# Two preparation steps of a cross-attention stage moved within a hand-written order (one core)

## The chip, the cores and the metric

The kernel runs on one core of a Trainium2 chip. The metric is the device time of one execution in microseconds (us), the median over several executions. Lower is better.

## The reference

The reference is a transformer of fourteen stages in float32 on 256 tokens of width 1024. Eight stages are gated feed-forward layers, four are token mixers of different kinds, and two are cross-attentions to a memory of 256 rows. Only the two cross-attentions (kind "xa", layers 0 and 1) are touched here:

```python
def memory_cross_attention(h, m, w_q, w_kv, q_gain, k_gain, w_o):
    q = rms_norm((h @ w_q).reshape(b, s, X_HEADS, X_HEAD_DIM), q_gain)
    kv = (m @ w_kv).reshape(b, m.shape[1], 2, X_HEADS, X_HEAD_DIM)
    k = rms_norm(kv[:, :, 0], k_gain)
    v = kv[:, :, 1]
    sc = jnp.einsum('bqhd,bkhd->bhqk', q, k).astype(jnp.float32) * (X_HEAD_DIM ** -0.5)
    p = jax.nn.softmax(sc, axis=-1).astype(v.dtype)
    o = jnp.einsum('bhqk,bkhd->bqhd', p, v).reshape(b, s, X_HEADS * X_HEAD_DIM)
    return o @ w_o
```

It is called with `h = rms_norm(x, xa_norm)` and `m = rms_norm(mem, xa_mem_norm)`. There are 4 heads of width 256.

## The kernel before, in words

**Tiles and precision.** All weights come as one stream of 829 tiles of 128x1024 in the order of use. SyncE loads them into four raw buffers (L421); a raw buffer is free once the tile in it is split. ScalarE casts a tile to its high part (`w_hi`, L1053), VectorE subtracts to get the low part (`w_lo`, L1487), and TensorE forms a product from three matmuls (high by high, high by low, low by high, L461). A projection tile ("w") is 8 chunks of 3 matmuls, 24 in all. The split parts lie in a ring of six, so TensorE can have several tiles ready ahead of it. Activations are split in the same way: a "high" on ScalarE (L1074) and a "low" on VectorE (L1514), chunk by chunk (8 chunks of 128 rows by 256 tokens).

**One list, five engines.** Each engine walks the same list of units from `before(kind, layer)`, and then, within the attention, one short list per group from `between(kind, layer)`. Each engine does its own share of a unit, strictly in the list's order, and engines meet only at semaphores. The units that matter here:

- `mh` c: the high (ScalarE) and low (VectorE) parts of chunks c and c+1 of the memory, written to the buffer "b". TensorE does nothing for it.
- `start` (kind "trio"): three query tiles at once, chunk by chunk, then the sum of squares of x; ScalarE takes its square root, VectorE the reciprocal `rstd_x` (L1506) and the three evacuations (L1732).
- `w` / `wk`: one projection tile. TensorE multiplies; VectorE evacuates it (L1716) and then splits the weight tile four places ahead; ScalarE casts that tile. `wk(0)` is the first tile that reads the memory's parts: TensorE waits before each of its 8 chunks for that chunk's low part.
- `hs`: ScalarE squares two evacuated tiles (L1241). `hn`: TensorE sums these squares over the head (it waits for `hs`), ScalarE takes the root (L1259), VectorE the reciprocal (L1774) and scales the two tiles (L1780, L1782).
- `vh`: half of a value tile; ScalarE evacuates after the second half (L1191).
- `att`: the attention's first step. On TensorE it is the scores of group 0, on VectorE their maximum (L1818, L1819), on ScalarE their exponentials (L1285).

In the attention, ScalarE does for each group g first the exponentials of group g+1, then the units of the group's list, then the copy of the transposed probabilities (L1297). TensorE does first the scores of group g+1 or g+2, then the same units, then the transposes (L823):

```python
                exps(0)
                yield
                for g in range(len(groups)):
                    if g + 1 < len(groups):
                        exps(g + 1)
                    for u in fill[g]:
                        unit(*u)
```

Before the change the list of an "xa" stage has the four `mh` units first, ahead of the trio. The squares of the last key head, `hs(*k(3))`, stand in `before` between `wk(7)` and the first half value tile, and its `hn` stands in the first list of `between`.

Of the kernel before, what the change touches and what calls it, by code (L numbers as in the profile page):

```python
# [141 lines left out]
def build(nc, stream_d, x_d, mem_d, vec_d, con_d, biasa_d, biasc_d, heads_d, out_d, stages=STAGES):  # L142
    total = sum(TILES[s] for s, _ in stages)
    with ExitStack() as ctx:
        def sb(name, shape, dt=F32):
            return ctx.enter_context(nc.sbuf_tensor(name, shape, dt))
# [14 lines left out]
        v = sb("v", [P, 2, D])  # L161
# [157 lines left out]
        def before(kind, layer):  # L319
            def hs(name, i, a, b):  # L320
                return ("hs", name, i, layer, a, b)

            def hn(name, i, a, b):
                return ("hn", name, i, layer, a, b)

            def w(k, *where):
                return ("w", "a", "x", k, *where)

            def start(*tiles):
                return ("trio", "a", "x", tiles, (T_BANK, 0, 2) if kind == "xa" else None)  # L330
            def hb(name, *pairs):
                return ("hb", name, layer, pairs)

            def vh(i, half):
                return ("vh", "a" if kind == "odd" or kind == "even" else "b", "x" if kind in ("odd", "even") else "m", v, i, half)
            if kind == "even":
                return [start(0, 1, 2), w(3, 0), hs("evq", 0, 0, 1), w(4, 1), ("col", "x"), hn("evq", 0, 0, 1),
                        hs("evq", 1, 2, 3), vh(0, 0), hn("evq", 1, 2, 3), hs("evk", 0, 4, 4), vh(0, 1), hn("evk", 0, 4, 4),
                        ("mem",), vh(1, 0), hb("evq", (0, 0, 1), (1, 2, 3)), vh(1, 1), hb("evk", (0, 4, 4)), ("stat", "m"),
                        vh(2, 0), ("col", "m"), ("att",), vh(2, 1)]  # L340
            if kind == "odd":
                def q(i):
                    return ("odq", i, 2 * i, 2 * i + 1)

                def k(i):
                    return ("odk", i, 2 * i + 8, 2 * i + 9)
                return [start(0, 1, 2), w(3, 0), hs(*q(0)), w(8, 1), ("col", "x"), w(9), hs(*q(1)), hn(*q(0)), w(10),
                        hn(*q(1)), w(11), hs(*k(0)), hb("odq", q(0)[1:], q(1)[1:]), w(4), hs(*k(1)), hn(*k(0)), w(5),
                        hn(*k(1)), w(6), hs(*q(2)), hb("odk", k(0)[1:], k(1)[1:]), w(7), w(12), ("att",), hs(*q(3)), hn(*q(2)), w(13),
                        hn(*q(3)), w(14), hs(*k(2)), hb("odq", q(2)[1:], q(3)[1:]), w(15), vh(0, 0), hs(*k(3)), hn(*k(2))]  # L350
            if kind == "xa":
                def q(i):
                    return ("xaq", i, 8 + 2 * i, 9 + 2 * i)

                def k(i):
                    return ("xak", i, 2 * i, 2 * i + 1)

                def wk(i):
                    return ("w", "b", "m", i)
                return [*(("mh", c, layer) for c in (0, 2, 4, 6)), start(8, 9, 10), w(11, 1), hs(*q(0)), w(12, 3), hs(*q(1)),  # L360
                        w(13), hn(*q(0)), w(14), hn(*q(1)), hs(*q(2)), w(15), wk(0), hn(*q(2)),
                        hs(*q(3)), wk(1), wk(2), hn(*q(3)), hs(*k(0)), wk(3), wk(4), hn(*k(0)), hs(*k(1)), wk(5), wk(6),
                        hs(*k(2)), hn(*k(1)), ("att",), wk(7), hs(*k(3)), vh(0, 0), hn(*k(2))]
            return ([start(0, 1, 48), w(2, 0), w(3, 1), ("col", "x")]
                    + [w(k) for k in range(4, 12)] + [("att",)] + [w(k) for k in range(12, 16)] + [("v", "a", "x", v, i) for i in range(4)])

        def between(kind, layer):

            if kind == "even":
                return [[("w", "a", "x", 5 + 2 * g), ("w", "a", "x", 6 + 2 * g)] for g in range(4)]  # L370
            if kind == "odd":
                out = [[("vh", "a", "x", v, (g + 1) // 2, (g + 1) % 2)] for g in range(7)] + [[]]
                out[0].append(("hn", "odk", 3, layer, 14, 15))
                out[1].insert(0, ("hb", "odk", layer, ((2, 12, 13), (3, 14, 15))))
                return out
            if kind == "xa":
                k3 = ("xak", 3, layer, 6, 7)
                return [[("vh", "b", "m", v, 0, 1), ("hn", *k3)]] + [[("v", "b", "m", v, g)] for g in range(1, 4)]
            rest = [("w", "a", "x", 16 + k) for k in range(8)] + [("v", "a", "x", v2, i) for i in range(4)]
            rest += [("w", "a", "x", 24 + k) for k in range(8)]  # L380
            return [rest[2 * g:2 * g + 2] for g in range(4)] + [rest[8 + 3 * g:11 + 3 * g] for g in range(4)]
# [62 lines left out]
        def _(pe):  # L444
# [311 lines left out]
            def attention(kind, layer):  # L756
# [4 lines left out]
                last_group = len(groups) - 1  # L761
                base = dict((s, t.so_far(s)) for s in (max_done, exp_done, p_ready, a_ready, pt_ready, o_lo, o_out))
                fill = between(kind, layer)

                def scores(g):
# [202 lines left out]
            def mixer(kind, layer):  # L968
# [4 lines left out]
                for u in before(kind, layer):  # L973
                    unit(*u)
# [53 lines left out]
        def _(act):  # L1028
# [233 lines left out]
            def attention(kind, layer):  # L1262
# [3 lines left out]
                cols = 2 * T if kind == "xa" else T + P  # L1266
                base = dict((s, t.so_far(s)) for s in (max_done, recip_done, tr_done, o_done))
                fill = between(kind, layer)
                into = "a" if kind == "xa" else "b"

# [114 lines left out]
            def mixer(kind, layer, following):  # L1385
# [4 lines left out]
                for u in before(kind, layer):  # L1390
                    unit(*u)
                    if kind == "mix" and u[0] == "w" and u[3] == 5:
                        gates()
                    if u[0] == "mem":
                        act.wait_ge(mem_loaded, 32)
                        for c in range(C):
                            square(c, mem[:, c, :])
# [72 lines left out]
        def _(dve):  # L1470
# [332 lines left out]
            def attention(kind, layer):  # L1803
                groups = groups_of(kind)
                nm = len(groups[0]["maps"])
                n_sets = 1 if kind in ("xa", "mix") else 2
                base = dict((s, t.so_far(s)) for s in (s_mm, exp_done, tr_done, o_hi, a_part, recip_done))
                fill = between(kind, layer)
                into = "a" if kind == "xa" else "b"

# [188 lines left out]
            def mixer(kind, layer, following):  # L1999
# [3 lines left out]
                for u in before(kind, layer):  # L2003
                    unit(*u)
                    if u[0] == "mem":
                        add_squares()
                    if kind == "mix" and u[0] == "w" and u[3] in (4, 8, 10):
                        gates(layer, (4, 8, 10).index(u[3]))
# [345 lines left out]
```

## Time and profile before

| what | value |
|---|---|
| median of three runs | 2628.57 us (2623.86 to 2634.04) |
| the profiled execution: its own time | 2623.86 us |
| its span in the profile | 2622.1 us |
| TensorE (PE) busy | 2545.0 us, 97% |
| VectorE (DVE) busy | 1802.4 us, 69% |
| ScalarE (ACT) busy | 1396.5 us, 53% |
| GpSimd (POOL) busy | 190.6 us, 7% |
| bytes moved | 445.89 MB, mean 170 GB/s |

PE is TensorE's matmuls, PEld its weight loads, PEclk the clock that TensorE was granted as a share of full speed. A timeline row gives the start in us from the span's start, the duration, the engine, the line of the kernel, the operation and its operands; in brackets stands the idle time of the engine just ahead of it and what ended that.

### The profile page before, as it was taken

What the parts mean: (1) busy time and instruction counts of PE and PEld (TensorE: products, weight loads), DVE (VectorE), ACT (ScalarE), POOL (GpSimd) and SP (SyncE); (2) the same over time, 40 slices, a digit from 0 to 9 for tenths busy, and PEclk for the clock granted to TensorE, in tenths of its full rate; (3) what the DMA queues carried; (4) which work ended last, traced back from release to release, by engine and by line L of the source; (5) the groups of instructions that cost most, each with busy time, mean ns of one, the idle gap of its engine ahead of it and who ended that gap; (6) DMA issues with size and microseconds to landing.
All of it is one profiled execution on the core that took longest, in us unless ns stands there. A gap on an engine that the chain in (4) does not pass through costs nothing.

```text
span 2622.1 us, 56431 instructions
## 1 busy us (share of the span) xinstructions
PE 2545.0 (97%) x21370; PEld 2468.5 (94%) x21370; DVE 1802.4 (69%) x2868; ACT 1396.5 (53%) x2232; POOL 190.6 (7%) x265
## 2 busy tenths in 40 slices
PE   8999799999999999999999999999999989999998
PEld 8998699999998899999998998989989989989998
DVE  6667686667667585767667657786686676676865
ACT  5456556445445655545445555654454465555543
POOL 0001001000000201000000250000000005300000
PEclk9999899999999999999999999999999999999999
DMA  7664244765564344655654543545545545335553
GB/s 270 208 192 137 81 145 157 234 211 188 195 194 155 105 164 142 201 193 180 203 193 147 182 146 113 169 161 185 184 161 192 193 147 174 129 115 176 175 193 113
DMA packets 122826, 445.89 MB, mean 170 GB/s; under 512 B 13688, under 2 KB 14712, under 8 KB 122688
## 3 DMA queue, kind: packets, MB, share of 16 engines
q1 hardware_dynamic: 120816, 436.79, 50.8%
q0 software_dynamic: 1872, 7.17, 0.8%
q8 instruction: 98, 1.61, 0.3%
q14 instruction: 40, 0.33, 0.0%
HBM read 442.86 MB, written 1.05 MB: 169 GB/s over the span
## 4 chain that ended last, share of the span: by engine, by line
PE 92%; DVE 5%; ACT 2%; issue 1%; DMA 0%; SPq 0%; DVEq 0%; ACTq 0%
PE bank L461 91%; DVE w_lo L1487 1%; PE bank L823 1%; DVE x L1558 1%; ACT w_hi L1053 1%; DVE z L1598 0%; DVE rstd_x L1506 0%; DVE x L1602 0%; DVE rstd_m L1553 0%; DVE score L1547 0%; DVE a L1514 0%; DMA raw<-in_stream_dram 0%; ACT score L1285 0%; DVE score L1538 0%; DVE z L1902 0%
## 5 line engine op out<-in xcount | busy, mean ns | idle before, releaser
L461 PE MATMUL bank<-a,w_hi 128*128 128x256 f32 x7472 | 1311.2, 280 | 37.6 <-DVE a L1514 28.0
L461 PEld LDWEIGHTS bank<-a,w_hi 128*128 128x128 f32 x7472 | 1137.1, 189 | 52.1 <-issue 47.4
L1487 DVE TENSOR_TENSOR w_lo<-raw,w_hi 128x1024 fp32r<-128x1024 f32 x829 | 1012.6, 1225 | 212.4 <-ACT w_hi L1053 210.8
L461 PE MATMUL bank<-a,w_lo 128*128 128x256 f32 x3736 | 1039.0, 278 | 0.0
L1053 ACT CAST w_hi<-raw 128x1024 fp32r<-128x1024 f32 x829 | 842.3, 1045 | 57.3 <-DMA raw<-in_stream_dram 53.8
L461 PE MATMUL bank<-b,w_hi 128*128 128x256 f32 x4800 | 839.3, 278 | 1.0 <-DVE b L1487 1.0
L461 PEld LDWEIGHTS bank<-b,w_hi 128*128 128x128 f32 x4800 | 726.8, 188 | 8.5 <-issue 3.6
L461 PEld LDWEIGHTS bank<-a,w_lo 128*128 128x128 f32 x3736 | 707.7, 189 | 0.0
L461 PE MATMUL bank<-b,w_lo 128*128 128x256 f32 x2400 | 664.9, 277 | 0.0
L461 PEld LDWEIGHTS bank<-b,w_lo 128*128 128x128 f32 x2400 | 451.4, 188 | 0.0
L1113 ACT CAST b<-hmid 128x256 fp32r<-128x256 f32 x132 | 53.8, 407 | 401.0 <-PE bank L461 389.7
L1625 DVE TENSOR_TENSOR hmid<-bank,rstd_x 128x256 f32<-128x256 f32 x168 | 71.2, 424 | 163.6 <-PE bank L461 163.5
L1109 ACT ACTIVATE sil<-sil 128x256 f32<-128x256 f32 x176 | 73.6, 418 | 145.7 <-DVE sil L1620 145.7
L1487 DVE TENSOR_TENSOR b<-hmid,b 128x256 fp32r<-128x256 f32 x132 | 56.0, 425 | 128.3 <-ACT b L1113 128.3
L461 PE MATMUL bank<-w_hi,a 128*128 128x256 f32 x736 | 130.7, 281 | 0.0
L2163 POOL TENSOR_SCALAR score<-score,rr 128x128 f32<-128x128 f32 (+1 forms) x96 | 44.5, 479 | 1114.7 <-DVE rr L1842 817.5
L461 PEld LDWEIGHTS bank<-w_hi,a 128*128 128x128 f32 x736 | 111.9, 188 | 3.4 <-issue 2.5
L1716 DVE TENSOR_TENSOR z<-bank,rstd_x 128x256 f32<-128x256 f32 x125 | 52.8, 422 | 79.0 <-PE bank L461 78.4
L461 PE MATMUL bank<-w_lo,a 128*128 128x256 f32 x368 | 102.2, 278 | 0.0
L1113 ACT CAST a<-hmid 128x256 fp32r<-128x256 f32 x44 | 17.9, 407 | 136.1 <-PE bank L461 132.5
L1639 DVE TENSOR_TENSOR hmid<-sil,hmid 128x256 f32<-128x256 f32 x176 | 74.8, 425 | 5.7
L1620 DVE TENSOR_TENSOR sil<-bank,rstd_x 128x256 f32<-128x256 f32 x160 | 67.8, 424 | 12.7 <-PE bank L461 2.8
(193 smaller groups left out, 1897.1 us busy)
## 6 DMA issues: line engine op xcount, KB each, us to landing
raw<-in_stream_dram SPq DMA_DIRECT2D x829, 512.0 KB, 3.7
z<-in_biasc_dram POOLq DMA_DIRECT2D x6, 512.0 KB, 4.9
z<-in_biasa_dram POOLq DMA_DIRECT2D x3, 512.0 KB, 4.7
x<-in_x_dram SPq DMA_DIRECT2D x2, 512.0 KB, 8.0
v<-in_mem_dram POOLq DMA_DIRECT2D x2, 512.0 KB, 5.9
out_dram<-x SPq DMA_DIRECT2D x8, 128.0 KB, 1.8
con<-in_con_dram POOLq DMA_DIRECT2D x1, 912.0 KB, 6.6
vec<-in_vec_dram POOLq DMA_DIRECT2D x1, 417.0 KB, 5.6
```

Source lines behind the costliest of these rows:

```text
L461: return nc.tensor.matmul(out, lhsT, rhs, start=start, stop=stop, skip_group_check=shared)
L823: last = nc.tensor.transpose(out[:, col:col + P], p[:, src:src + P], ident)
L1053: nc.scalar.copy(w_hi[:, slot, :], raw[:, raw_slot, :]).then_inc(hi_split, 1)
L1109: nc.scalar.activation(sil[:, jj, :], sil[:, jj, :], ACT.Silu).then_inc(silu_done, 1)
L1113: nc.scalar.copy(high_of["b"][:, jj, :], hmid[:, jj, :]).then_inc(hhi_done, 1)
L1487: return nc.vector.tensor_tensor(out, a, hi.bitcast(F32), ALU.subtract)
L1558: ins = nc.vector.tensor_tensor(x[:, c, :], x[:, c, :], rstd["m"][:, :], ALU.mult)
L1620: nc.vector.tensor_tensor(sil[:, j % 2, :], gate_up_of(j, after_mixer)[0], r, ALU.mult)\
L1625: nc.vector.tensor_tensor(hmid[:, j % 2, :], gate_up_of(j, after_mixer)[1], r, ALU.mult)\
L1639: nc.vector.tensor_tensor(hmid[:, jj, :], sil[:, jj, :], hmid[:, jj, :], ALU.mult)\
L1716: nc.vector.tensor_tensor(z[:, tile, :], out[:, 0:T], rstd[norm][:, :], ALU.mult).then_inc(w_evac, 1)
L2163: last = nc.gpsimd.tensor_scalar(p, p, rr[:, k, b:b + 1], 1.0, ALU.mult, ALU.mult)
```

## The change

Three edits in the lists, for both "xa" stages. The four `mh` units leave the front of `before`: the first now stands behind `hn(*q(0))`, the second behind `hs(*q(2))`, the third and fourth behind `w(15)`, directly ahead of `wk(0)`. And `hs(*k(3))` leaves `before` and becomes the first unit of the first list of `between`, so that on ScalarE it comes behind the exponentials of group 1.

```diff
-                return [*(("mh", c, layer) for c in (0, 2, 4, 6)), start(8, 9, 10), w(11, 1), hs(*q(0)), w(12, 3), hs(*q(1)),
-                        w(13), hn(*q(0)), w(14), hn(*q(1)), hs(*q(2)), w(15), wk(0), hn(*q(2)),
+                return [start(8, 9, 10), w(11, 1), hs(*q(0)), w(12, 3), hs(*q(1)), w(13), hn(*q(0)), ("mh", 0, layer), w(14),
+                        hn(*q(1)), hs(*q(2)), ("mh", 2, layer), w(15), ("mh", 4, layer), ("mh", 6, layer), wk(0), hn(*q(2)),
                         hs(*q(3)), wk(1), wk(2), hn(*q(3)), hs(*k(0)), wk(3), wk(4), hn(*k(0)), hs(*k(1)), wk(5), wk(6),
-                        hs(*k(2)), hn(*k(1)), ("att",), wk(7), hs(*k(3)), vh(0, 0), hn(*k(2))]
+                        hs(*k(2)), hn(*k(1)), ("att",), wk(7), vh(0, 0), hn(*k(2))]
...
             if kind == "xa":
                 k3 = ("xak", 3, layer, 6, 7)
-                return [[("vh", "b", "m", v, 0, 1), ("hn", *k3)]] + [[("v", "b", "m", v, g)] for g in range(1, 4)]
+                return [[("hs", *k3), ("vh", "b", "m", v, 0, 1), ("hn", *k3)]] + [[("v", "b", "m", v, g)] for g in range(1, 4)]
```

## Rows read from the trace of the kernel before

**Rows 1.** The page, part 1: busy time of each engine over the span.

```profile
PE 2545.0 (97%) x21370; PEld 2468.5 (94%) x21370; DVE 1802.4 (69%) x2868; ACT 1396.5 (53%) x2232; POOL 190.6 (7%) x265
```

**Rows 2.** Stretches of the two xa stages: busy time of each engine, granted clock, DMA.

```profile
324.50:385.40 60.90, 60.90 (x488) 59.39 (x487) 52.43 (x74) 33.32 (x51) 0.94 (x2) 1.00 0.48 156
926.40:987.20 60.80, 60.80 (x487) 59.33 (x486) 52.47 (x74) 33.50 (x51) 0.94 (x2) 1.00 0.47 157
```

**Rows 3.** The waits of TensorE over the whole span: total, times, longest.

```profile
PE bank L461 <- DVE w_lo L1487: 9.2, 8, 1.8
```

**Rows 4.** Timeline of VectorE, front of the first xa stage.

```profile
327.52 3.25 DVE L1514 SCALAR_TENSOR_TENSOR b<-v,vec,b 128x256 fp32r<-128x256 f32 x8
330.69 1.22 DVE L1487 TENSOR_TENSOR w_lo<-raw,w_hi 128x1024 fp32r<-128x1024 f32 x1
334.71 1.75 DVE L1506 RECIPROCAL rstd_x<-rstd_x 128x256 f32<-128x256 f32 x1 [2.80 <-ACT rstd_x L1068]
```

**Rows 5.** Timeline of ScalarE, same stage: memory highs, a late cast.

```profile
326.04 3.29 ACT L1074 ACTIVATE b<-v,vec 128x256 fp32r<-128x256 f32 x8
...
343.49 1.05 ACT L1053 CAST w_hi<-raw 128x1024 fp32r<-128x1024 f32 x1 [2.58 <-DMA raw<-in_stream_dram]
```

**Rows 6.** Timeline of VectorE, first xa stage, up to wk(0)'s evacuation.

```profile
344.58 1.23 DVE L1487 TENSOR_TENSOR w_lo<-raw,w_hi 128x1024 fp32r<-128x1024 f32 x1 [1.46 <-ACT w_hi L1053]
...
348.30 0.42 DVE L1716 TENSOR_TENSOR z<-bank,rstd_x 128x256 f32<-128x256 f32 x1
...
352.35 0.42 DVE L1716 TENSOR_TENSOR z<-bank,rstd_x 128x256 f32<-128x256 f32 x1
...
353.81 0.42 DVE L1716 TENSOR_TENSOR z<-bank,rstd_m 128x256 f32<-128x256 f32 x1
```

**Rows 7.** Timeline of VectorE, the same place of the second xa stage.

```profile
944.88 1.23 DVE L1487 TENSOR_TENSOR w_lo<-raw,w_hi 128x1024 fp32r<-128x1024 f32 x1
...
952.64 0.42 DVE L1716 TENSOR_TENSOR z<-bank,rstd_x 128x256 f32<-128x256 f32 x1
```

**Rows 8.** DMA issues at 338.56, then at 940.38: size, us to landing.

```profile
raw<-in_stream_dram SPq DMA_DIRECT2D x1, 512.0 KB, 4.9
...
raw<-in_stream_dram SPq DMA_DIRECT2D x1, 512.0 KB, 3.4
```

**Rows 9.** Timeline of TensorE: wk(0)'s first matmuls, hn(q2)'s, hn(k3)'s, hn(q2)'s in the second stage.

```profile
349.38 0.39 PE L461 MATMUL bank<-b,w_hi 128*128 128x256 f32 x2
...
352.10 1.03 PE L461 MATMUL bank<-sil,con 128*128 128x256 f32 x4
...
384.53 1.02 PE L461 MATMUL bank<-hmid,con 128*128 128x256 f32 x4
...
953.93 1.03 PE L461 MATMUL bank<-sil,con 128*128 128x256 f32 x4
```

**Rows 10.** Chain that ended last at 301.83: VectorE's end to TensorE's start.

```profile
301.83 0.14 issue
```

**Rows 11.** Timeline of ScalarE around hs(k3), first xa stage.

```profile
378.09 0.64 ACT L1241 ACTIVATE hmid<-z 128x512 f32<-128x512 f32 x1
...
379.69 1.28 ACT L1259 ACT_TABLE_LOAD   x1
...
385.33 0.47 ACT L1285 ACTIVATE score<-bank,nmx 128x256 f32<-128x256 f32 x1 [2.57 <-DVE nmx L1819]
...
386.24 1.04 ACT L1053 CAST w_hi<-raw 128x1024 fp32r<-128x1024 f32 x1
```

**Rows 12.** Timeline of VectorE: the reciprocal of hn(k2), first xa stage.

```profile
381.49 1.75 DVE L1774 RECIPROCAL rt<-rt 128x256 f32<-128x256 f32 x1 [0.56 <-ACT rt L1259]
```

**Rows 13.** Timeline of TensorE after two pauses of other stages.

```profile
865.32 0.52 PE L823 MATMUL bank<-con,score 128*128 128x128 f32 x3 [1.64 <-ACT pt L1297]
...
1721.26 0.76 PE L461 MATMUL bank<-a,w_hi 128*128 128x256 f32 x2 [3.81 <-DVE a L1514]
```

**Rows 14.** Stretches behind these pauses: columns as in rows 2.

```profile
868.00:871.00 3.00, 3.00 (x15) 2.77 (x14) 1.66 (x4) 2.99 (x10) 0.35 (x1) 0.50 0.00 0
...
1721.20:1724.20 3.00, 2.94 (x14) 2.97 (x15) 3.00 (x9) 2.06 (x7) 0.00 (x0) 0.50 0.00 0
```

## The prediction

> **What bounds the kernel now.** I read the page first: TensorE is busy for 97% of the span, so a change pays only where TensorE stands still, and costs wherever it makes TensorE stand still [rows 1]. Next came the stretches of the two stages that the change touches. From 324.5 us to the point where the attention's first transposes begin, TensorE is busy 60.90 of 60.90 us in the first stage and 60.80 of 60.80 us in the second, at the full granted clock [rows 2]. The view of waits, asked for 322 to 426 us and for 924 to 1028 us, lists no wait of TensorE at all. So the old order costs TensorE nothing, and there is no idle time there for the new order to win back. The question is only whether the new order makes TensorE wait. For that I read the timelines of VectorE and ScalarE, because the moved units run on these two alone, and laid them beside TensorE's.
>
> **Edit 1, what it removes.** At the front, eight highs on ScalarE take 3.29 us [rows 5] and eight lows on VectorE 3.25 us [rows 4]. The next instruction starts 3.17 us after the first low, so one low takes up 3.17 / 8 = 0.40 us of VectorE and lasts 3.25 - 7 x 0.40 = 0.48 us from start to result. TensorE is in the 72 matmuls of the trio then. Behind the lows VectorE does one weight split and then waits 2.80 us for the root, which waits for TensorE's own sum of squares [rows 4]. The 3.2 us that the edit frees therefore end in that wait: it becomes about 6 us, and everything after it starts when it did. The removal is worth nothing; its cover was the trio.
>
> **Edit 1, what it adds.** The same lows now stand in the stretch between `hn(q0)` and `wk(0)`, where VectorE has no pause. In the first stage its last wait is the one before 344.58 (1.46 us, for a late cast), and from there to 353.81 it goes from one instruction to the next [rows 6]. It is also already behind TensorE: `w(15)` is evacuated at 352.35 [rows 6], although TensorE left that tile for `wk(0)` at 349.38 [rows 9]. Today this lag of 3.0 us hurts nobody, since `wk(0)` needs nothing that VectorE makes in it. After the edit it does, because the last four memory chunks come behind that evacuation. Step by step, first stage:
>
> - `mh` 0 behind `hn(q0)` pushes the evacuation of `w(14)` from 348.30 to 349.10. Chunks 0 and 1 are ready just in time for TensorE at 349.38.
> - `mh` 2 behind `hn(q1)` adds another 0.80: the evacuation of `w(15)` goes from 352.35 to 353.95. Chunk 2, wanted at 350.06, is ready at about 353.6.
> - The evacuation and the split that belongs to it take 353.81 - 352.35 = 1.46 us [rows 6], so `mh` 4 starts at 355.41.
> - Chunk 7 starts three lows later, at 356.60, and is ready at 357.08. The handover to TensorE takes 0.14 us [rows 10], its three matmuls 3 x 0.113 = 0.34 us (24 matmuls in 352.10 - 349.38 = 2.72 us [rows 9]). TensorE reaches `hn(q2)` at 357.56 instead of 352.10: **5.5 us late**.
>
> In the second stage VectorE doesn't wait at this place (944.88 carries no bracket) and evacuates `w(15)` at 952.64 [rows 7]. The same steps give 952.64 + 1.60 + 1.46 + 1.19 + 0.48 + 0.14 + 0.34 = 957.85 against 953.93 [rows 9]: **3.9 us late**. The 1.5 us between the stages come from one weight tile that landed 4.9 us after its issue in the first stage and 3.4 us in the second [rows 8]; ScalarE waited 2.58 us for it [rows 5]. I take the two stages as the trace has them, 9.4 us; both on time gives 7.9, both late 11.0. ScalarE's highs are no limit: it idles 2.58 us just ahead, and each pair of highs (0.8 us) is done before VectorE reaches the lows. Everything on TensorE is queued behind `wk(0)`, and as it has no idle time later in the stage, none of this comes back. VectorE, in contrast, recovers its lag while TensorE stands, so I expect no second wait in `wk(1)` to `wk(7)`.
>
> A rule of the Trainium skill bears on the late tile. "DMA: Bandwidth & Descriptors", section "Anatomy of one DMA", gives a transfer as about 2.0 us plus its bytes over 436 GB/s, fitted on the software queue; for 512 KB that makes an estimate of 3.2 us. The trace's 3.4 agrees roughly and its 4.9 doesn't. By the page both stages would be on time, and the sum below would be 14.6 instead of 16.1.
>
> **Edit 2.** Before, ScalarE does the squares of k3 at 378.09, 0.53 us of its time, and TensorE wants them only at 384.53 [rows 9, 11]. Taking them out lets the next cast, the table load of 1.28 us and the root of `hn(k2)` go 0.53 us earlier. VectorE's reciprocal waits for just that root [rows 12], so the maximum and then the exponentials of group 1, which wait for the maximum, move from 385.33 to 384.80. The exponentials take 386.24 - 385.33 = 0.91 us, so the squares now start at 385.71 and end 0.64 us later; with 0.14 us of handover TensorE has them at 386.49 instead of needing them at 384.53: **2.0 us late**. Behind TensorE's wait in `hn(k3)` stand the first transposes and the scores of group 2. ScalarE's next cast starts at 386.24, as before, so the later engines keep their times and have more room. The second stage repeats the pattern (the stretch differs by 0.1 us [rows 2]): 2 x 1.96 = 3.9 us. No table load is added: the squares already stand behind exponentials in the trace and need none.
>
> **The clock.** The granted clock fell to 0.50, the lower level of 1.2 GHz, after pauses of TensorE of this size: after 1.64 us with a second short pause behind it at 865, and after 3.81 us at 1721 [rows 13, 14]; four further places with a pause of over 3 us look the same. In 3.0 us at that level it did 14 and 15 matmuls, where 0.113 us each gives 26, so a stretch costs at least 1.5 us. In `wk(0)` TensorE pauses for about 3.6 and 1.5 us in the first stage, for about 2.1 and 1.5 us in the second. The nearest rows say the clock falls in both. Some 0.17 us of the loss hides behind VectorE's pace of 0.40 us for a chunk that takes TensorE 0.34. I take 1.4 us for each stage, 2.8 us; the bounds are 0 and 3.4. [...]
>
> **Sum.** 9.4 + 3.9 + 2.8 = 16.1 us on the profiled execution's own 2623.86 us, which is 2640.0 us. That execution lies 4.7 us below the median, so against the median of 2628.57 us I expect **2644.7 us**, 0.61% slower. About 0.5%, 13.1 us, is what a measurement of this kernel can tell from no change; the three runs before spread over 10.2 us.
>
> **The rivals.**
>
> - *The waits come, the clock holds or every tile is on time.* Without the clock's term the sum is 13.3, and with both tiles on time as well 11.8; with the clock's term and both tiles on time it is 14.6, still in the forecast. For it: the pauses of the second stage are shorter than most of those behind which the clock fell. It ends at 2640 to 2642, on the edge of 0.5%.
> - *Only one edit costs.* If `hs(k3)` slips in unnoticed, 12.2 is left; if the memory lows do, 3.9. Against it: both terms are three to ten times the error of the durations they are made of.
> - *Not slower.* The lows would have to be ready when TensorE asks. TensorE wants chunk 4 at 349.38 + 4 x 0.34 = 350.74 and I have it at 356.0, so VectorE's chain would have to run about 5 us earlier. The only thing that frees VectorE by such an amount is the empty front (3.2 us), and that is cut off by the wait for the root [rows 4]. If that wait were shorter than it looks, the weight splits would run ahead instead and TensorE would lose at most its waits for `w_lo` elsewhere, 9.2 us in all [rows 3]. So this gives 0 to -9 us, which is not over 0.5% either. For it speaks only that a trace is one execution.
> - *Worse.* Late tiles in both stages (+1.6), a clock that falls again behind the 2.0 us pause of `hn(k3)` (+1.5 each): up to 21 us, 2650.
> - *The change does nothing to the order.* Not possible for VectorE and ScalarE, which walk the list strictly; TensorE has no share in `mh` and `hs`, so its own order is unchanged.
>
> **How the numbers follow.** Forecast (both waits and at least one fall of the clock, 13.2 to 19 us) 0.50; the clock holds or all is on time below that, 0.20; one edit only 0.13; not slower 0.10; worse 0.07. Slower by over 0.5% is the forecast, worse, and a little of the second case: 0.60. Within 0.5%: 0.37. Faster by over 0.5%: 0.03. The range runs from 2634 to 2653 us: it takes in the forecast and the clock's case with the scatter of a median (some 4 us), the upper half of "one edit only", and half of "worse".
>
> **What the profile would show.** A wait of TensorE on the low parts at L1514 in both stages, two pauses in `wk(0)` summing to about 5 and 4 us; no wait of TensorE at the front; a wait of TensorE for ScalarE's squares at L1241 of about 2 us in both stages; a granted clock of 0.50 for some 3 us just behind `wk(0)`'s pauses; VectorE waiting about 6 us for the first root. Wrong would be: no L1514 wait in these stretches (the lag of VectorE was mis-read), or a wait of TensorE in `wk(1)` to `wk(7)` (VectorE does not catch up).

## The result, and the profile after

The changed kernel takes 2650.11 us (median of five runs, 2643.33 to 2652.35), the kernel before 2632.77 us in the same comparison (median of five). The ratio is 1.0067 with a 95% interval of 1.0044 to 1.0090: 0.67% slower, where 0.61% was forecast. 2650.11 us lies inside the range of 2634 to 2653 us. Over all 22 executions of the changed kernel on record (2639.14 to 2661.78 us) the median is 2646.1 us.

The profiled execution of the changed kernel spans 2637.3 us against 2622.1 us. Part 1 of its page, to be read beside [rows 1]: VectorE and ScalarE do what they did before to within 0.2 us, and TensorE executes the same 21370 matmuls.

```profile
PE 2550.8 (97%) x21370; PEld 2472.8 (94%) x21370; DVE 1802.2 (68%) x2868; ACT 1396.5 (53%) x2232; POOL 190.6 (7%) x265
```

The waits of TensorE over the whole span (total us, times, longest). Against the kernel before, the waits on the low parts at L1514 grew by two on buffer "a" and two on "b" (before there were 28.0 us in 6 on "a" and none on "b"), and the waits on ScalarE's squares at L1241 went from 0.3 us in one to 3.7 us in three. The waits for `w_lo` are 8.4 us instead of 9.2 [rows 3]. Outside the two stages a wait of 0.7 us for an evacuation at L1716 is new.

```profile
PE bank L461 <- DVE a L1514: 31.0, 8, 11.0
...
PE bank L461 <- DVE w_lo L1487: 8.4, 8, 1.8
...
PE bank L461 <- ACT hmid L1241: 3.7, 3, 1.7
...
PE bank L461 <- DVE b L1514: 3.3, 2, 2.7
```

Timeline of VectorE, first xa stage of the changed kernel. It answers to [rows 4, 6]. The wait for the root is 5.99 us instead of 2.80, and the reciprocal starts 1.57 us behind the start of TensorE's sum-of-squares matmul (332.82), as before (334.71 against 333.14): the front gave nothing. From 343.47 VectorE has no pause until the last low, and `w(15)` is evacuated at 352.82.

```profile
334.39 1.75 DVE L1506 RECIPROCAL rstd_x<-rstd_x 128x256 f32<-128x256 f32 x1 [5.99 <-ACT rstd_x L1068]
...
343.47 1.23 DVE L1487 TENSOR_TENSOR w_lo<-raw,w_hi 128x1024 fp32r<-128x1024 f32 x1 [0.67 <-ACT w_hi L1053]
...
347.20 0.87 DVE L1514 SCALAR_TENSOR_TENSOR b<-v,vec,b 128x256 fp32r<-128x256 f32 x2
...
352.03 0.88 DVE L1514 SCALAR_TENSOR_TENSOR b<-v,vec,b 128x256 fp32r<-128x256 f32 x2
352.82 0.42 DVE L1716 TENSOR_TENSOR z<-bank,rstd_x 128x256 f32<-128x256 f32 x1
353.16 1.21 DVE L1487 TENSOR_TENSOR w_lo<-raw,w_hi 128x1024 fp32r<-128x1024 f32 x1
354.29 1.66 DVE L1514 SCALAR_TENSOR_TENSOR b<-v,vec,b 128x256 fp32r<-128x256 f32 x4
357.79 0.42 DVE L1716 TENSOR_TENSOR z<-bank,rstd_m 128x256 f32<-128x256 f32 x1 [1.83 <-PE bank L461]
```

Timeline of TensorE, the pauses of both stages: chunk 2 and chunk 4 of `wk(0)`, then `hn(k3)` [rows 9]. The start of `wk(0)` itself, 349.07, is on time.

```profile
349.07 0.39 PE L461 MATMUL bank<-b,w_hi 128*128 128x256 f32 x2
...
352.56 0.80 PE L461 MATMUL bank<-b,w_hi 128*128 128x256 f32 x2 [2.65 <-DVE b L1514]
...
354.82 0.80 PE L461 MATMUL bank<-b,w_hi 128*128 128x256 f32 x2 [0.60 <-DVE b L1514]
...
392.44 1.13 PE L461 MATMUL bank<-hmid,con 128*128 128x256 f32 x4 [1.70 <-ACT hmid L1241]
...
963.86 0.50 PE L461 MATMUL bank<-a,w_hi 128*128 128x256 f32 x2 [1.90 <-DVE a L1514]
...
966.12 0.63 PE L461 MATMUL bank<-a,w_hi 128*128 128x256 f32 x2 [1.24 <-DVE a L1514]
...
1003.50 1.13 PE L461 MATMUL bank<-hmid,con 128*128 128x256 f32 x4 [1.70 <-ACT hmid L1241]
```

Stretches of the changed kernel, columns as in [rows 2]: the granted clock (third figure from the right) is 0.50 behind the pauses of `wk(0)` and 1.00 behind the pause of `hn(k3)`. In the first stage it is down already when the first pause ends, and the two first rows together are 6.0 us at 0.50; in the second stage it is down for about 3.4 us.

```profile
352.60:355.60 3.00, 2.40 (x9) 2.10 (x10) 3.00 (x7) 0.00 (x0) 0.00 (x0) 0.50 0.07 11
355.60:358.60 3.00, 3.00 (x14) 2.82 (x13) 1.17 (x3) 0.00 (x0) 0.00 (x0) 0.50 0.47 164
966.40:969.40 3.00, 3.00 (x14) 2.91 (x14) 1.33 (x5) 0.00 (x0) 0.00 (x0) 0.50 0.52 175
393.50:396.50 3.00, 3.00 (x21) 2.79 (x20) 1.70 (x2) 2.80 (x5) 0.00 (x0) 1.00 0.28 66
```

**The yardstick of the experiments.** The time of one execution scatters by some 20 us, so most experiments are read on one stretch in each stage: from the trio's sum-of-squares matmul to the first transposes of the attention. It holds everything that the change touches. In the changed kernel's timeline it runs from the first to the second of these rows, and from the third to the fourth: 60.59 and 59.59 us. In the kernel before it is 52.25 us in both stages (333.14 to 385.39, 934.97 to 987.22). The change adds 8.34 + 7.34 = 15.7 us there. Where the table below has no ratio, the kernel was executed once, and only the stretches are read.

```profile
332.82 0.38 PE L461 MATMUL bank<-score,con 128*128 128x256 f32 x1
...
393.41 0.38 PE L823 MATMUL bank<-con,score 128*128 128x128 f32 x2
...
944.88 0.38 PE L461 MATMUL bank<-score,con 128*128 128x256 f32 x1
...
1004.47 0.38 PE L823 MATMUL bank<-con,score 128*128 128x128 f32 x2
```

| kernel | stage 1, us | stage 2, us | clock at 0.50 behind wk(0)'s pause | ratio (95%) |
|---|---|---|---|---|
| before | 52.25 | 52.25 | no, no | |
| after | 60.59 | 59.59 | yes, yes | 1.0067 (1.0044 to 1.0090) |
| after, once more | 60.34 | 60.95 | yes, yes | |
| memory parts only | 59.42 | 58.86 | yes, yes | 1.0045 (1.0026 to 1.0064) |
| squares only | 54.23 | 54.23 | no, no | 1.0007 (0.9986 to 1.0027) |
| all four at wk(0) | 58.39 | 57.45 | yes, yes | |
| two in front, two late | 56.75 | 54.58 | yes, no | |
| all four behind the trio | 53.83 | 53.83 | no, no | |
| squares behind vh(0,0) | 52.25 | 52.25 | no, no | |
| after, pauses filled | 59.49 | 58.14 | no, no | |

### The profile page after: what moved, and what is told of

It reads as the page before. It is cut to its first block, busy times and chain, and to the rows that moved or that the text cites. A ratio compares the mean times of both kernels' runs of the same rounds, so it can differ in the third digit from the quotient of the medians.

```text
span 2637.3 us, 56431 instructions
## 1 busy us (share of the span) xinstructions
PE 2550.8 (97%) x21370; PEld 2472.8 (94%) x21370; DVE 1802.2 (68%) x2868; ACT 1396.5 (53%) x2232; POOL 190.6 (7%) x265
## 4 chain that ended last, share of the span: by engine, by line
PE 89%; DVE 7%; ACT 3%; issue 1%; DMA 1%; SPq 0%; DVEq 0%; ACTq 0%
PE bank L461 88%; DVE w_lo L1487 1%; ACT w_hi L1053 1%; PE bank L823 1%; DVE rt L1774 1%; DVE x L1558 1%; DVE rstd_x L1506 0%; DMA raw<-in_stream_dram 0%; DVE z L1598 0%; DVE score L1547 0%; ACT score L1285 0%; DVE a L1514 0%; DVE rstd_m L1553 0%; DVE x L1602 0%; DMA x<-in_x_dram 0%
## 5 line engine op out<-in xcount | busy, mean ns | idle before, releaser
L1716 DVE TENSOR_TENSOR z<-bank,rstd_x 128x256 f32<-128x256 f32 x125 | 52.6, 421 | 78.1 <-PE bank L461 77.4
```

Of the source, the lines that this page charges most:

```text
L1716: nc.vector.tensor_tensor(z[:, tile, :], out[:, 0:T], rstd[norm][:, :], ALU.mult).then_inc(w_evac, 1)
```

## The experiments

**1. Edit 1 alone.** The list of `before` as changed, `hs(*k(3))` back in its old place:

```diff
-                        hs(*k(2)), hn(*k(1)), ("att",), wk(7), vh(0, 0), hn(*k(2))]
+                        hs(*k(2)), hn(*k(1)), ("att",), wk(7), hs(*k(3)), vh(0, 0), hn(*k(2))]
...
-                return [[("hs", *k3), ("vh", "b", "m", v, 0, 1), ("hn", *k3)]] + ...
+                return [[("vh", "b", "m", v, 0, 1), ("hn", *k3)]] + ...
```

> The memory parts moved as in the change; the squares of k3 stay where they were. The measure for each xa stage is the stretch from the trio's sum-of-squares matmul to the first transposes, 52.25 us in both stages before, 60.6 and 59.6 us after. Theory (two independent waits, each of its own edit): TensorE's two pauses in wk(0) stay, the wait on ScalarE's squares is gone, so the stretches are about 58.6 and 57.6 us (one tile that lands late moves the one or the other by up to 1.6 us); in all about 12 us slower than before, ratio 1.0045. Rival (the two waits share a cause, so that one edit alone costs little or nearly all of it): under 3 us or over 14 us.

Measured: ratio 1.0045 (1.0026 to 1.0064), stretches of 59.42 and 58.86 us, no wait on L1241. Each wait belongs to its own edit, and the ratio is the expected one. The stretches are 0.8 and 1.3 us longer than expected. In the first stage 0.5 us of this is the late tile (ScalarE waits 2.27 us for it, 1.79 in the changed kernel's profile). In the second stage the clock tells why: it is at 0.50 for over 6 us, not for some 3:

```profile
963.00:966.00 3.00, 2.64 (x12) 2.64 (x13) 1.50 (x4) 0.00 (x0) 0.00 (x0) 0.50 0.49 175
966.00:969.00 3.00, 3.00 (x12) 2.64 (x11) 2.01 (x3) 0.96 (x3) 0.00 (x0) 0.50 0.00 0
```

**2. Edit 2 alone.** The kernel before with only `hs(*k(3))` moved as in the change.

> Only hs(k3) moved; the memory parts stay in front. Theory: TensorE waits about 2.0 us for ScalarE's squares in both stages and nowhere else in them, stretches of 54.2 us, in all 3.9 us slower, ratio 1.0015. The pause is alone, so the clock stays up. Rival (the wait in the changed kernel exists only because VectorE and ScalarE were thrown off by the first edit): no wait, 52.25 us. Rival (such a pause brings the clock down): 55.5 us or more.

Measured: 54.23 us in both stages, that is +1.98 each, one wait of 1.7 us on L1241 in each, the clock at 1.00, ratio 1.0007 (0.9986 to 1.0027). The wait belongs to this edit and needs nothing of the other. The 4.0 us are not told from zero by the total, whose interval is 5 us to either side; the stretch tells them. The row is the same in both stages:

```profile
PE bank L461 <- ACT hmid L1241: 1.7, 1, 1.7
```

**3. All four units at wk(0).** Edit 1 alone, with the lows collected at its last place:

```diff
-w(13), hn(*q(0)), ("mh", 0, layer), w(14), hn(*q(1)), hs(*q(2)), ("mh", 2, layer), w(15), ("mh", 4, layer), ("mh", 6, layer), wk(0)
+w(13), hn(*q(0)), w(14), hn(*q(1)), hs(*q(2)), w(15), *(("mh", c, layer) for c in (0, 2, 4, 6)), wk(0)
```

> All four mh units directly ahead of wk(0), none between hn(q0) and w(15); squares of k3 as before the change. Theory (what counts is all the work that VectorE has to do up to the last low, wherever in that stretch the lows stand): chunk 7 is ready at the same time as in the first experiment, so the stretches are the same within 0.5 us apart from a late tile, with one long wait on L1514 at the first chunk (about 4.5 to 5 us in a stage with a late tile, 3.0 to 3.5 without) and TensorE then keeping VectorE's pace. Rival (the lows cost by pushing the evacuations of w(14) and w(15)): no pushing, so 1.6 us less for each stage.

Measured: one wait on L1514 in each stage, 4.4 and 3.3 us, stretches of 58.39 and 57.45 us. That is 1.0 and 1.4 us under experiment 1, two to three times the 0.5 us that the theory allowed, and in the rival's direction. The timelines of VectorE in the first stage separate the two; the first two rows are experiment 1, the last two this one. From the end of VectorE's last pause to the end of the last low it is 353.33 + 1.67 - 342.51 = 12.49 us there and 352.12 + 3.25 - 342.89 = 12.48 us here.

```profile
342.51 1.23 DVE L1487 TENSOR_TENSOR w_lo<-raw,w_hi 128x1024 fp32r<-128x1024 f32 x1 [1.16 <-ACT w_hi L1053]
...
353.33 1.67 DVE L1514 SCALAR_TENSOR_TENSOR b<-v,vec,b 128x256 fp32r<-128x256 f32 x4
...
342.89 1.22 DVE L1487 TENSOR_TENSOR w_lo<-raw,w_hi 128x1024 fp32r<-128x1024 f32 x1 [0.94 <-ACT w_hi L1053]
...
352.12 3.25 DVE L1514 SCALAR_TENSOR_TENSOR b<-v,vec,b 128x256 fp32r<-128x256 f32 x8
```

So the lows are ready at the same time. TensorE doesn't keep VectorE's pace of 0.40 us a chunk at first: the clock has fallen in its long wait (0.50 from 353 to 355 us), and the five chunks from 352.75 on take 0.6 to 0.8 us each. But the clock is back up sooner than in experiment 1. The row below lies 22.7 to 25.7 us behind the second stage's sum-of-squares matmul (940.33) and has 0.91; the two rows of experiment 1 lie 20.9 to 26.9 us behind it (942.13) and have 0.50. The length of the fall was not set by this experiment, so that it makes up all of the 1.0 and 1.4 us is an inference.

```profile
963.00:966.00 3.00, 3.00 (x22) 2.90 (x22) 1.31 (x2) 0.45 (x2) 0.00 (x0) 0.91 0.00 0
```

**4. Two units in front, two at wk(0).**

```diff
+                return [("mh", 0, layer), ("mh", 2, layer), start(8, 9, 10), ...
+                        hn(*q(1)), hs(*q(2)), w(15), ("mh", 4, layer), ("mh", 6, layer), wk(0), hn(*q(2)),
```

> mh 0 and 2 in front as before, mh 4 and 6 directly ahead of wk(0); squares of k3 as before the change. Theory: VectorE has 1.6 us less to do before chunk 7, so the delay of wk(0) falls from about 5.5 and 3.9 us (late tile, no late tile) to 3.9 and 2.3 us, stretches of 54.5 to 56.2 us if the clock holds and up to 1.5 us more if it falls; one wait on L1514, at chunk 4, of 2.0 to 3.7 us. Rival (the distance of the last two units from wk(0) is what counts): as in the first experiment, 57.6 us or more.

Measured: one wait on L1514 of 2.6 us in the first stage and 1.9 us in the second; stretches of 56.75 and 54.58 us. The second stage shows the bare delay, since the clock held: 54.58 - 52.25 = 2.33 us against the 2.3 us worked out. With half of the lows left in front VectorE has 1.6 us less to do, and the bare delay is 3.9 - 2.3 = 1.6 us less: one for one. In the first stage the clock fell behind the 2.6 us.

**5. All four units behind the trio.**

```diff
-                return [*(("mh", c, layer) for c in (0, 2, 4, 6)), start(8, 9, 10), w(11, 1), ...
+                return [start(8, 9, 10), *(("mh", c, layer) for c in (0, 2, 4, 6)), w(11, 1), ...
```

> All four mh units directly behind the trio; squares of k3 as before the change. Theory (VectorE's lag behind TensorE is the resource that is spent): the lows are ready long before wk(0), so no wait on L1514, but the 3.2 us push VectorE's evacuations, and wk(0) and wk(1), which need the banks of w(14) and w(15), wait about 1.2 and 0.6 us for VectorE's evacuations at L1716; stretches of about 54 us. Rival (only a wait for the lows themselves can cost): 52.25 us.

Measured: 53.83 us in both stages, no wait on L1514, and waits on VectorE's evacuations at L1716, of TensorE at `wk(0)` (0.85 us idle) in both stages and at `wk(1)` (0.17 us, the second row) in the second. The rival is out: even lows that are ready in time cost 1.6 us a stage, because they stand before the evacuations that TensorE needs. The single waits were worked out as 1.2 and 0.6 us, a bit too long; in the first stage no wait shows at `wk(1)`, though the stretch is as long.

```profile
952.98 0.50 PE L461 MATMUL bank<-a,w_hi 128*128 128x256 f32 x2 [0.85 <-DVE z L1716]
...
957.03 0.50 PE L461 MATMUL bank<-a,w_hi 128*128 128x256 f32 x2 [0.17 <-DVE z L1716]
```

**6. The squares one unit later instead of behind the exponentials.**

```diff
-                        hs(*k(2)), hn(*k(1)), ("att",), wk(7), hs(*k(3)), vh(0, 0), hn(*k(2))]
+                        hs(*k(2)), hn(*k(1)), ("att",), wk(7), vh(0, 0), hs(*k(3)), hn(*k(2))]
```

> Only hs(k3) moved, and only behind vh(0,0), still ahead of hn(k2)'s root and of the exponentials of group 1. Theory (the squares are late because ScalarE's exponentials of group 1, which wait for VectorE's maximum, stand ahead of them): no wait on L1241, stretches of 52.25 us. Rival (any later place costs, because ScalarE is short there): a wait of 0.5 us or more.

Measured: 52.25 us in both stages and no wait of TensorE in them. It is the exponentials ahead of the squares that make them late, not the later place as such. Timeline of ScalarE: the squares at 380.75 end well before the exponentials of group 1 at 387.04.

```profile
380.75 0.63 ACT L1241 ACTIVATE hmid<-z 128x512 f32<-128x512 f32 x1
...
387.04 0.48 ACT L1285 ACTIVATE score<-bank,nmx 128x256 f32<-128x256 f32 x1 [2.57 <-DVE nmx L1819]
```

**7. The pauses filled.** The changed kernel, with matmuls into an unread bank ahead of the waits for chunks 2 and 4 of `wk(0)`:

```diff
+                    def chunk_ready(c):
+                        for _ in range({2: 16, 4: 8}.get(c, 0)):
+                            mm(bank[0][:, 0:T], filler[:, 0, 0:P], filler[:, 1, :], True, True)
+                        wait_chunk(c)
```

> The changed kernel with extra matmuls on TensorE in wk(0), 16 ahead of the wait for chunk 2 and 8 ahead of the wait for chunk 4, written to a bank that nothing reads; the computation is unchanged. At full clock they take 1.8 and 0.9 us and fit in the pauses. Theory (the fall of the clock is a cost of its own, brought about by the pauses): the granted clock stays at 1.0 in both stages and the stretches are about 59.4 and 58.2 us, 1.2 to 1.4 us shorter than in the changed kernel, apart from a late tile. Rival (the clock falls whatever TensorE does there, or its fall is hidden by VectorE's pace): no shorter.

Measured: 59.49 and 58.14 us, the clock at 1.00 behind the pauses in both stages. Against the changed kernel that is 1.1 and 1.45 us less. The first stage had a later weight tile (ScalarE waited 2.37 us for it, 1.79 in the changed kernel's profile), so at equal landing it is about 1.7 (1.10 + 2.37 - 1.79). In both stages the fall went when the pauses were filled, and the time with it: the fall comes from the pauses and is a cost of its own.

```profile
356.00:359.00 3.00, 3.00 (x24) 2.90 (x23) 2.28 (x5) 0.63 (x2) 0.00 (x0) 1.00 0.52 180
968.00:971.00 3.00, 3.00 (x29) 3.00 (x28) 2.96 (x4) 2.88 (x4) 0.00 (x0) 1.00 0.33 85
```

**8 and 9. Pauses filled at the stage boundaries.** If a filled pause keeps the clock up, the kernel before should gain where its clock falls today. Both start from the kernel before and add float32 matmuls behind the last sum of squares of a stage. There are five such places (the expectation of the first says seven, a slip; it lists the five), and one such matmul takes 0.43 us, not 0.86.

```diff
+            def fill(out, n):
+                for _ in range(n):
+                    mm(out[:, 0:T], ones, strict[:, 0:T], True, True)
...
                     sum_of_parts()
+                    if k < 7:
+                        fill(bank[5], 6)
...
                 sum_chunk(C - 1)
+                fill(bank[0], 8)
```

> The kernel before, with three extra float32 matmuls (0.86 us each, written to a bank that nothing reads; the computation is unchanged) on TensorE at seven stage boundaries, behind the last sum of squares of the feed-forward stages 4 to 6 and of the two mixers of kind mix, where TensorE pauses 3.5 to 4.2 us for the next stage's first low part. Theory (a pause filled as in the previous experiment keeps the granted clock up, and its fall costs about 1.6 us a place): the falls at 1407, 1721, 1919, 2127 and 2424 us of the kernel before are gone, the pauses themselves stay as long as they were, 5 x 1.6 = 8 us faster, ratio 0.997. Rival (the clock falls there for other reasons, or the fill delays the first matmul of the next stage): the falls stay, ratio 1.000 or above.

> As the previous experiment, with more fill: six extra float32 matmuls behind the feed-forward stages 4 to 6 and eight behind the two mixers of kind mix (0.43 us each by the previous run, where three of them shortened a pause of 3.47 us to 2.18 us), so that under 0.6 us of each pause is left. Theory (the falls are brought about by the pauses, and the two that came up at 1429 and 2132 us in the previous run come from pauses that were filled by half only): no fall between 1395 and 2460 us, the first matmul of the next stage as early as before, about 8 us faster than the kernel before, ratio 0.997. Rival (the falls move to the next pauses, which are not filled): falls stay at 1429 or 2132 us, ratio 0.999 or above.

Measured: with three matmuls at each place the ratio is 0.9987 (0.9968 to 1.0005), with six and eight 0.9989 (0.9973 to 1.0005). The 0.997 that the theory named lies just inside the first interval and just outside the second, and neither tells a gain from none. In the profile of the first, two falls are left, at 1429 and 2132 us. In the profile of the fuller one the falls at 1407, 1721, 1919, 2127 and 2424 us are all gone and only one is left between 1395 and 2460 us, at 2455, so the clock did what the theory says. The time followed only in part. Timeline of TensorE with the full fill at the first place, where the two first rows stand for a pause of 3.09 us and for none before:

```profile
1406.73 0.47 PE L461 MATMUL bank<-a,w_hi 128*128 128x256 f32 x2 [0.50 <-DVE a L1521]
...
1420.00 0.47 PE L461 MATMUL bank<-a,w_hi 128*128 128x256 f32 x2 [1.22 <-DVE w_lo L1494]
...
1423.36 0.60 PE L461 MATMUL bank<-con,rstd_x 1*128 1x1 f32 x4 [0.30 <-DVE rstd_x L1513]
...
1425.38 0.47 PE L461 MATMUL bank<-a,w_hi 128*128 128x256 f32 x2 [1.41 <-DVE w_lo L1494]
```

From the first low part to 1425 TensorE needs 1425.38 - 1406.73 = 18.65 us with the clock up and needed 1425.19 - 1406.54 = 18.65 us with the clock down. What it gains at full clock it waits away 13 us later for a weight split of VectorE (1.22 us). At this place VectorE's chain behind the boundary sets the pace, and a slow TensorE was free.

At the other places some of the time came back. The rows are TensorE at the place of 1721 us, before [rows 13] and then with the full fill: 1737.39 - 1721.26 = 16.13 us against 1737.50 - 1721.89 = 15.61, so 0.5 us. The same reading gives 0.7 us at 1919 (1917.60 to 1933.85 before, 1917.70 to 1933.29 filled), and 0.5 us at 2424, there up to VectorE's next `rstd_x` (2424.44 to 2436.73 before, 2428.20 to 2439.99 filled).

```profile
1737.39 0.47 PE L461 MATMUL bank<-a,w_hi 128*128 128x256 f32 x2 [0.27 <-DVE w_lo L1487]
...
1721.89 0.47 PE L461 MATMUL bank<-a,w_hi 128*128 128x256 f32 x2 [0.35 <-DVE a L1521]
...
1737.50 0.47 PE L461 MATMUL bank<-a,w_hi 128*128 128x256 f32 x2 [0.52 <-DVE w_lo L1494]
```

The whole 1.6 us came back only at 2127, from a wait of 1.41 us on TensorE to an evacuation on VectorE: 2147.71 - 2126.76 = 20.95 us before, 2151.47 - 2132.14 = 19.33 us with the fill.

```profile
2126.76 0.47 PE L461 MATMUL bank<-a,w_hi 128*128 128x256 f32 x2 [1.41 <-DVE w_lo L1487]
...
2147.71 0.42 DVE L1716 TENSOR_TENSOR z<-bank,rstd_x 128x256 f32<-128x256 f32 x1 [0.75 <-PE bank L461]
...
2132.14 0.47 PE L461 MATMUL bank<-a,w_hi 128*128 128x256 f32 x2 [1.41 <-DVE w_lo L1494]
...
2151.47 0.42 DVE L1723 TENSOR_TENSOR z<-bank,rstd_x 128x256 f32<-128x256 f32 x1 [0.58 <-PE bank L461]
```

Together that is 0 + 0.5 + 0.7 + 1.6 + 0.5 = 3.3 us of the 8 expected, read from one profile of each kernel. It would be a ratio of 0.9987, which lies inside both intervals. The waits for `w_lo` over the span grew from 9.2 to 12.2 us. Whether the fill took away the fall at 2127 is open: before, the clock was at 1.00 from the end of the 3.09 us pause at 2108 on and fell 19 us later behind short waits (1.06, 0.38 and 1.41 us), and those short waits are still there in the filled kernel. No version here is shown to beat the kernel before.

**10. The changed kernel once more.**

> The changed kernel once more, to see what differs from execution to execution in the two stages. Theory (the chain is fixed but for the landing of one weight tile and the length of the clock's fall): the wait on L1241 is 1.7 us and the pauses before chunks 4 are 1.0 to 1.5 us again; the stretches lie between 58.1 us (no late tile, no fall) and 61.5 us (late tile, long fall). Rival (the 60.6 and 59.6 us were chance): outside of that.

Measured: 60.34 and 60.95 us, the wait on L1241 again 1.7 us, the pause before chunk 4 1.24 us in both. In the first stage that is new, for the changed kernel's first profile had 0.60 us there, with the clock already down. Both stretches lie between the two bounds.

## Why the prediction was right

- *No gain at the front.* Shown: the wait for the root grew from 2.80 to 5.99 us.
- *Edit 1, 5.5 and 3.9 us.* In the second stage 7.34 us in all, less 1.98 for edit 2 and 1.45 for the clock (experiment 7), leaves 3.9 us, as forecast. In the first 8.34 - 1.98 - 1.7 leaves 4.7 us. The weight tile landed late again but by 0.8 us less (ScalarE waited 1.79 instead of 2.58 us), and 5.5 - 0.8 = 4.7. In the first stage this tile took 4.1 us or more from issue to landing in all twelve profiles. The Trainium skill, "DMA: Bandwidth & Descriptors", section "Anatomy of one DMA", gave an estimate of 3.2 us, by a fit for the software queue; for this transfer it is at least 0.9 us too short. That the delay follows from all of VectorE's work up to the last low is shown by experiments 3, 4 and 5: where the lows stand in the stretch changes where TensorE waits; how many stand in it changes for how long.
- *The pauses in `wk(0)`.* Two in each stage, as forecast, but 2.65 + 0.60 = 3.3 and 1.90 + 1.24 = 3.1 us long, not about 5 and 4. In the first stage 0.8 us of the difference is the tile. Another part is that TensorE took longer for the chunks between the pauses: chunk 4 starts 2.26 us behind chunk 2 in both stages, and of these the profile counts 1.66 us as busy in the first stage, where the clock is down by then, and 1.02 us in the second. The forecast counted 6 x 0.113 = 0.68 us of work there. The delay of `wk(0)` doesn't depend on how the 2.26 us are divided, so the sum doesn't suffer.
- *Edit 2, 2.0 us each.* 1.98 us in both stages when alone (experiment 2); with edit 1 the same wait of 1.7 us shows. Experiment 6 shows the cause.
- *The clock, 1.4 us each.* 1.45 us in the second stage and about 1.7 in the first at equal landing (experiment 7). The working was less exact than the result. By their counts the stretches of [rows 14] cost (26 - 15) x 0.113 = 1.2 and (26 - 14) x 0.113 = 1.4 us, not at least 1.5. Of the four further places named with a pause of over 3 us, one doesn't look the same: behind the 3.09 us pause at 2108 the clock held, and it fell at 2127 behind short waits. And no row shows the bound of 3.4 us for both stages. The fall can be twice as long as assumed: where it was so in the second stage (experiments 1 and 10), the stretch was 1.3 and 1.4 us longer.
- *The sum.* 16.1 us forecast; 15.7 us in the two stretches of the profile; 0.67% of 2632.77 us is 17.6 us. Some of the closeness is luck: the tile was 0.8 us less late than in the first stage's term, and the clock cost 0.3 us more there. The interval of the ratio (11.6 to 23.7 us) is far wider than what separates these.
- *No wait in wk(1) to wk(7).* Right: VectorE waits 1.83 us for TensorE at the end of `wk(0)`, its lag is gone.

What was sized too short is the scatter. I put it down to medians as some 4 us; single executions of one kernel differ by up to 23 us (2639.14 to 2661.78 of the changed kernel), and the median of the kernel before was 2628.57 us over three of them and 2632.77 over five. What this is made of stands below.

## What to carry to other kernels

Before moving a step on an engine that works in order, don't ask how busy that engine is but how late it is against the engine that sets the end, at each place: VectorE was idle for a third of the span and 3.0 us behind just where the work was put. Work that waits ahead of a forced wait (here the root of the first norm) is free and should stay there; behind it, each instruction pushes all that follow. And a pause of the bound engine costs more than itself when the clock falls behind it, but winning the clock back pays only as far as that engine, and not the one that feeds it, sets the pace afterwards: here 3.3 us of the 8 expected, over five places.

## What the runs showed of the hardware

- The granted clock fell to 0.50 behind two pauses with idle times of 1.90 and 1.24 us and six matmuls between them (second stage of the changed kernel), and stayed at 1.00 behind a single pause of 1.70 us (`hn(k3)`) in both stages of all four profiles that have it. Of two single pauses in experiment 4, one of 2.61 us brought it down and one of 1.88 us did not. The Trainium skill, "TensorE: Matmul & The Clock Gate", section "HAM oscillation", tells of a kernel that waits about 3 to 5 us for data in every turn of its loop and finds the clock down each time; here it also fell behind pauses that are shorter than that.
- The largest part of the scatter that the profiles show is the pace of the matmuls in the last three feed-forward stages. Each of these stages runs in one execution at 0.113 us a matmul and in another at 0.118, at a granted clock of 1.00 both times, and it holds for the whole stage. The first two rows are the kernel before, two of these stages: 140 us / 1191 = 0.118, 140 / 1237 = 0.113.

```profile
1760.00:1900.00 140.00, 140.00 (x1191) 140.00 (x1190) 85.79 (x116) 61.38 (x83) 0.00 (x0) 1.00 0.58 191
...
2460.00:2600.00 140.00, 140.00 (x1237) 140.00 (x1236) 89.78 (x121) 63.73 (x87) 0.00 (x0) 1.00 0.57 185
```

The repeated execution of the changed kernel, last stage, at the slower pace:

```profile
2480.00:2620.00 140.00, 140.00 (x1190) 140.00 (x1190) 90.88 (x123) 64.44 (x87) 0.00 (x0) 1.00 0.60 197
```

A feed-forward stage has 66 x 24 = 1584 such matmuls, so the slower pace costs 1584 x 0.0044 = 7 us a stage. The profile of before had one such stage, that of after none, and its repeat three (span 2657.2 us, 19.9 us more). The kernel of experiment 6, whose two stages are as fast as before, had three and spans 2642.3 us. So the 15.2 us between the two first spans agree with the 15.7 us of the two stretches partly by chance: the faster pace of one stage is offset by further falls of the clock elsewhere. What decides the pace was not found; the first five feed-forward stages ran at 0.113 us in all twelve profiles.
